# A decoder layer on one core: the per-layer embedding's projection moved from the routing to the place after the last expert

## The chip, the cores and the metric

The kernel runs on one core of a Trainium2 chip. The metric is the device time of one execution in microseconds (us). Lower is better. The core has a tensor engine (PE; PEld is its weight load), a vector engine (DVE), a scalar engine (ACT), a gather and scatter engine (POOL) and a queue engine (SP) that issues most of the transfers (DMAs).

## What is computed

One layer for 512 prompt tokens and 8 sample tokens (520 rows of 1024 numbers, float32):

```
h = x @ w_in                      # latents, rotary key, conv input, two gates
A = conv module,  B = latent attention, output projection to 1024
x = LN1(alpha*x + (sigmoid(gA)*A + sigmoid(gB)*B) @ w_out)
x = LN2(alpha*x + HierMoE(x))     # best of 4 groups, then best 2 of its 8 experts, SwiGLU
ple = sigmoid(x @ w_ple_gate) * (p @ w_ple_proj)      # p: 520 x 256, w_ple_proj: 256 x 1024
x = x + RMSNorm(ple) * ple_norm_g
```

The product `p @ w_ple_proj` is the per-layer embedding's projection. It depends on no other stage: its inputs are an input tensor and a weight. Only the last stage, called the tail here, reads its result.

## The kernel before

All engines work on one big SBUF tensor, `arena`, in which the offsets `A_...` give every buffer its place; `ps` is the PSUM with its eight banks of 512 columns. The program of each engine is written out by hand, in the order in which the engine executes it, and semaphores (`s_...`, `m....`) tie the engines together. Nothing reorders the work.

The rows are treated in five tiles: four of 128 rows and one of 8. `ORDER` (8-row tile first) is the order around the first layer norm, `ORDER2` (a full tile first, then the 8-row tile) the one in the tail. The program has these stages:

1. Input products, convolution, sample attention, prompt attention, output projection (up to line 1079).
2. Product with `w_out`, first layer norm on DVE, turning of each tile to `x1T` (`turn_x1`, L1085), and the routing's logits (`logits_x1`, L1095). The products with 36 columns go to bank 6.
3. Routing (L1930 to L2043): DVE finds the group and the experts, PE counts (L1142, L1144) and later places the tokens (L1156). `R_IDX` on the semaphore `s_r` says that the row indices are there. POOL then gathers the rows of the first block pair (L2203).
4. Experts: 18 passes over 16 pairs of experts. In each, `rows_in` turns the gathered rows (L1171), `gate_up` multiplies them with the two experts' weights (L1180), `turn_h` (L1187) and `down` (L1200) follow. The weights lie in three slots (`wx[0..2]`), which SP refills as they come free (L633): gate and up weights of pair k when the `gate_up` of the slot's last use is over (L668), down weights after its `down` (L674). POOL gathers rows and scatters results to DRAM (L2210).
5. A loop over experts that overflow (`overflow`, L549), which every engine runs through. Here no block overflows. When POOL is through, it raises `s_ovd` (L2241), and every engine waits for that.
6. Tail: SP loads the scattered results and the saved rows again (L708, L709). ACT scales each tile's first choice (`first_choice`, L1494), DVE adds up and normalizes (`front`: L2091, L2094 and `norm`, L1866 to L1876, with a root on ACT, L1499), PE turns the tile (`turn_x2`, L1240) and multiplies with `w_ple_gate` (L1265, L1273), ACT takes the sigmoid (L1514), DVE multiplies with the projection, and so on.

The projection is done by `ple_rows(u)` on PE (L1130), four products of 512 columns for a tile, which PE executes as eight MATMUL instructions since the data are float32. They go to banks 0 to 3, and ACT copies them to `x1` (`ple_out`, L1446), whose rows have been stored to DRAM by then. The calls stand between the steps of stages 2 and 3:

```
logits_x1(TILES - 2)
ple_rows(0)
turn_x1(TILES - 1)
logits_x1(TILES - 1)
ple_rows(1)
```

`ple_rows(2)` stands after the counting, `ple_rows(3)` and `ple_rows(4)` after the placing (L1156) and before the first `rows_in`, which also waits until ACT has emptied the banks. The weight `wpp` lies in the place of the buffer `yb` and is loaded by SP between the weights of slot 0 and of slot 1.

Of the kernel before, what the change touches and what calls it, by code (L numbers as in the profile page):

```python
# [14 lines left out]
P = 128  # L15
D = 1024
# [38 lines left out]
EW = EW1 + 2 * D  # L55
TILES = 5
ROWS = [P, P, P, P, NS]

ORDER = [4, 0, 1, 2, 3]
# [56 lines left out]
LN_STEPS, FD = 10, 8  # L116
# [80 lines left out]
A_W1 = A_OT  # L197
# [7 lines left out]
A_Y = A_W1 + 2 * EW  # L205
A_PLT = A_Y + 2048
assert A_PLT + 2 * T <= A_EXT
A_WPP = A_Y
A_PG = A_X1T

A_PLG = A_W1
A_ROWS = A_W1 + 8192
A_FX = A_W0
A_FBT = A_FX + TILES * D
A_SG = A_FBT + 2 * D
# [10 lines left out]
def decoder_layer(nc, a, o):  # L226

    ctx = ExitStack()
    with ctx:
# [7 lines left out]
        ps = ctx.enter_context(nc.psum_tensor("ps", [P, 8, 512], F32))  # L237
# [78 lines left out]
        wpp = at(A_WPP, 2 * D).rearrange("p (k n) -> p k n", k=2)  # L316
# [4 lines left out]
        plT = at(A_PLT, 2 * T).rearrange("p (k t) -> p k t", k=2)  # L321
# [142 lines left out]
        s_fd = sem("s_fd")  # L464
# [13 lines left out]
        s_plw = sem("s_plw")  # L478
        s_plg = sem("s_plg")
        s_pg = sem("s_pg")  # L480
        s_pp = sem("s_pp")
        s_ppe = sem("s_ppe")
# [78 lines left out]
        def _(sp):  # L561
# [75 lines left out]
                for x in range(2):  # L637
                    expert_weights(0, x, x, down)
            sp.wait_ge(s_mt, KD)
            sp.dma_start(wpp[:], a["w_plp"]).then_inc(s_plw, 16)  # L640
            sp.dma_start(plT[:], a["plT"]).then_inc(s_plw, 16)
            for down in range(2):
                for x in range(2):
# [35 lines left out]
            for k in range(3, EPAIRS):  # L679
# [5 lines left out]
                if k + 1 < EPAIRS and not early:  # L685
                    gate_up_weights(k + 1)
            sp.wait_ge(m.y, LAST_USE[EPAIRS - 3] + 1)
            sp.dma_start(plg[:], a["w_plg"]).then_inc(s_plg, 16)
            sp.dma_start(ln2r[:], a["lnrows"][:, 2:4]).then_inc(s_plg, 16)
            sp.wait_ge(s_r, R_STEPS)  # L690
# [14 lines left out]
            for u, t in enumerate(ORDER2):  # L705
                n = ROWS[t]
# [12 lines left out]
        def _(pe):  # L719
            mm = nc.tensor.matmul  # L720
# [380 lines left out]
            for u in range(1, TILES):  # L1101
                t, b = ORDER[u], 2 * (u % 2)
                if u >= 3:
                    pe.wait_ge(s_fd, FD * (u - 2) + 1)
                for k in range(KD):
# [4 lines left out]
                    for h in range(2):  # L1110
                        y = mm(ps[:, b + h, :], mixT[:, k, t * P:(t + 1) * P], wbig[:, k, h * 512:(h + 1) * 512],  # L1111
                               start=(k == 0), stop=(k == KD - 1))
# [1 line left out]
                if u >= 2:  # L1114
                    logits_x1(u - 2)
                turn_x1(u - 1)
            def ple_rows(u):

                t, b = ORDER[u], 2 - 2 * (u % 2)
                n = ROWS[t]  # L1120
                if u == 0:
                    pe.wait_ge(s_plw, 32)
                    pe.wait_ge(s_fd, FD * 3 + 1)
                elif u == 1:
                    pe.wait_ge(s_fd, FD * 4 + 1)
                else:
                    pe.wait_ge(s_ppe, u - 1)
                for k in range(2):
                    for h in range(2):
                        y = mm(ps[0:n, b + h, :], plT[:, k, t * P:t * P + n], wpp[:, k, h * 512:(h + 1) * 512],  # L1130
                               start=(k == 0), stop=(k == 1))
                y.then_inc(s_pp, 1)

            logits_x1(TILES - 2)
            ple_rows(0)
            turn_x1(TILES - 1)
            logits_x1(TILES - 1)
            ple_rows(1)


            pe.wait_ge(s_r, R_RANK)
            mm(ps[:, 7, 0:(TILES + 1) * 32], utri, ohs6.rearrange("p t e -> p (t e)"), start=True, stop=False)  # L1142
            for t in range(TILES):
                y = mm(ps[:, 7, 32 * (t + 1):32 * (TILES + 1)], ones, ohs[:, t:t + 1].to_broadcast([P, TILES - t, 32]),  # L1144
                       start=False, stop=(t == TILES - 1))
            y.then_inc(s_rp, 1)
            ple_rows(2)


            pe.wait_ge(s_rt2, 1)  # L1150
            for k in range(2):
                for t in range(TILES):
                    n = ROWS[t]
                    pe.wait_ge(s_rb, TILES * k + t + 1)
                    for x in range(2):
                        y = mm(ps[64 * x:64 * x + 64, 6, 0:SLOTS // P], inrow[0:n, k, t],  # L1156
                               inblk[0:n, k, t].rearrange("p (q x) -> p x q", x=2)[:, x],
                               start=(k == 0 and t == 0), stop=(k == 1 and t == TILES - 1))
            y.then_inc(s_rp, 1)


            ple_rows(3)
            ple_rows(4)

            def rows_in(p, xs, gathered):
                pe.wait_ge(s_xg[xs], gathered)
# [36 lines left out]


            pe.wait_ge(s_r, R_IDX)
            pe.wait_ge(s_ppe, TILES - 1)
            rows_in(0, 0, 16)
            pe.wait_ge(s_ppe, TILES)
            for p, (b, k) in enumerate(PASS):
                slot, n = weight_slot(k)  # L1210
                gate_up(p, slot, 32 * n)
# [2 lines left out]
                if p > 0:  # L1214
                    slot, n = weight_slot(PASS[p - 1][1])
# [17 lines left out]
            def turn_x2(u):  # L1233
                t = ORDER2[u]
                n = ROWS[t]
                pe.wait_ge(s_hf, HF_STEPS * (u + 1))
                if u >= 1:
                    pe.wait_ge(s_hc, 2 * u)
                for k in range(KD):
                    y = tr(ps[:, 4 + k // 4, (k % 4) * P:(k % 4) * P + n], fx[0:n, t, k * P:(k + 1) * P], ident[0:n, 0:n])  # L1240
                y.then_inc(s_ht, 1)

            pe.wait_ge(s_plg, 32)
            turn_x2(0)
            for u, t in enumerate(ORDER2):
                b = 2 * (u % 2)
                pe.wait_ge(s_hc, 2 * (u + 1))
                if u >= 2 and u != 3:
                    pe.wait_ge(s_hg, u - 1)
                if u == 1:  # L1250
                    narrow(6, lambda k: fbT[:, 1, k, 0:32], plg).then_inc(s_np, 1)
                elif u < TILES - 1:
                    for k in range(KD):
                        if k == KD // 2 and u == 0:
                            turn_x2(1)
                        if k == KD // 2 and u == 2:
                            pe.wait_ge(s_npc, 1)
                            narrow_sum(2, nparts, 1).then_inc(s_h, 1)
                            turn_x2(3)
                        if k == KD // 2 and u == 3:  # L1260
                            turn_x2(4)
                        if k == 0 and u == 3:
                            pe.wait_ge(s_hg, 2)
                        for h in range(2):
                            y = mm(ps[:, b + h, :], fbT[:, u % 2, k], plg[:, k, h * 512:(h + 1) * 512],  # L1265
                                   start=(k == 0), stop=(k == KD - 1))
                    y.then_inc(s_h, 1)
                    if u == 0:
                        turn_x2(2)
                else:  # L1270
                    for h in range(2):
                        for k in range(KD):
                            y = mm(ps[:, b + h, :], fbT[:, u % 2, k], plg[:, k, h * 512:(h + 1) * 512],  # L1273
                                   start=(k == 0), stop=(k == KD - 1))
                        y.then_inc(s_h, 1)
# [3 lines left out]
        def _(act):  # L1279
# [158 lines left out]

            def ple_out(u):

                t, b = ORDER[u], 2 - 2 * (u % 2)
                n = ROWS[t]
                act.wait_ge(s_pp, u + 1)
                act.wait_ge(s_fx, u + 1)
                act.wait_ge(s_x1[u], 16)
                av(x1[0:n, t], ps[0:n, b:b + 2, :].rearrange("p h n -> p (h n)"), ACT.Copy).then_inc(s_ppe, 1)  # L1446

            ple_out(0)
            x1_out(TILES - 1)

            act.wait_ge(s_r, R_EXP)
            av(gg[:], gx[:], ACT.Exp).then_inc(s_ra, 1)
            act.wait_ge(s_r, R_EXP2)
            av(gf, gf, ACT.Exp).then_inc(s_ra, 1)
            for u in range(1, TILES):
                ple_out(u)

            def rows_in(p):
                act.wait_ge(m.xt, p + 1)
# [56 lines left out]
            def squares(u):  # L1516
# [3 lines left out]
                act.wait_ge(s_hs, 2 * u + 1)  # L1520
                av(rms[0:n, 1:2], rms[0:n, 0:1], ACT.Sqrt, bias=eps[0:n, 0:1], scale=1.0 / D).then_inc(s_hs, 1)

            act.wait_ge(s_ovd, 1)
            for u in range(3):
                first_choice(u)
# [839 lines left out]
```

## Time and profile before

| | |
|---|---|
| median of 3 runs | 1042.96 us (1040.09 to 1043.85) |
| the profiled execution: its own time | 1042.33 us |
| span in its profile | 1040.6 us |
| PE busy | 937.9 us (90% of the span) |
| DVE, ACT, POOL busy | 422.9, 244.1, 94.4 us |
| moved by the DMAs | 244.08 MB, mean 235 GB/s |
| chain of work that ended last | PE 72%, DMA 14%, DVE 8%, ACT 3%, the rest queues and issue |

The span is what the profiler sees between the first and the last instruction; the execution's own time has 1.7 us around it. "Busy" says that an engine works on an instruction. It does not say that the time hangs on it: this is read from the chain of work that ended last, which goes back from the last instruction to what released it each time. The granted clock (PEclk) is 1.00 where TensorE has its 2.4 GHz and 0.50 where it has 1.2 GHz.

### The profile page before, as it was taken

Reading aid. Unit: us, or ns where it says so; the run is one execution under the profiler, and the core shown is the slowest. Engines: PE = TensorE matmul, PEld = TensorE weight load, DVE = VectorE, ACT = ScalarE, POOL = GpSimd, SP = SyncE. Lnnn points to the kernel's source line nnn. Section 1 sums busy time; section 2 is a strip of 40 time slices with the busy share of each in tenths; the row PEclk is TensorE's granted clock in tenths of the full one; section 3 lists DMA queues with packets and bytes.
Section 4 is the critical chain, followed back from the end, with each engine's and each line's share of the span. In section 5 each row is a group of like instructions: output and inputs, shape, how many; then the busy total and the mean of one; then the engine's idle time right before and its main releaser. Section 6 shows DMA issues by size and latency. Waiting matters only on the chain.

```text
span 1040.6 us, 13802 instructions
## 1 busy us (share of the span) xinstructions
PE 937.9 (90%) x5204; PEld 562.2 (54%) x5204; DVE 422.9 (41%) x934; ACT 244.1 (23%) x515; POOL 94.4 (9%) x143
## 2 busy tenths in 40 slices
PE   7999988999989989999899998889999987950996
PEld 6777766777767755665588444443333332320442
DVE  0211387565543247668512344452111111113773
ACT  0122121032224015766600000211111110101344
POOL 0111211211112000000000000011111111110000
PEclk9999998999999999999999999889999998995899
DMA  9766885996967500101125942329999999977001
GB/s 377 283 232 244 308 298 200 319 349 236 361 224 249 225 26 19 44 20 38 66 102 222 423 205 106 137 72 409 425 419 427 422 423 426 408 307 251 1 21 61
DMA packets 61221, 244.08 MB, mean 235 GB/s; under 512 B 10738, under 2 KB 11507, under 8 KB 51683
## 3 DMA queue, kind: packets, MB, share of 16 engines
q1 hardware_dynamic: 42818, 189.04, 46.6%
q0 software_dynamic: 13152, 35.28, 9.4%
q10 hardware_dynamic: 5184, 18.88, 4.8%
q8 instruction: 42, 0.69, 0.3%
q14 instruction: 25, 0.20, 0.1%
HBM read 239.69 MB, written 14.87 MB: 245 GB/s over the span
## 4 chain that ended last, share of the span: by engine, by line
PE 72%; DMA 14%; DVE 8%; ACT 3%; issue 2%; SPq 1%; ACTq 0%; DVEq 0%; POOLq 0%
PE ps L768 17%; DMA arena<-in_wexp 10%; PE ps L1180 8%; PE ps L1068 5%; PE ps L1111 5%; PE ps L1265 3%; PE ps L1200 3%; PE ps L856 3%; PE ps L761 3%; PE ps L827 3%; PE ps L937 2%; DMA arena<-in_state 2%; DVE arena L1747 2%; PE ps L961 2%; PE ps L1130 1%
## 5 line engine op out<-in xcount | busy, mean ns | idle before, releaser
L768 PE MATMUL ps<-arena 128*128 128x260 f32 x960 | 223.7, 389 | 6.1 <-DMA arena<-in_w 6.1
L768 PEld LDWEIGHTS ps<-arena 128*128 128x128 f32 x960 | 181.4, 193 | 40.7 <-issue 8.5
L1180 PE MATMUL ps<-arena 128*64 128x512 f32 x576 | 129.4, 602 | 16.0 <-DMA arena<-in_wexp 14.5
L1180 PEld LDWEIGHTS ps<-arena 128*64 128x64 f32 x576 | 42.7, 139 | 90.3 <-issue 88.4
L1599 DVE SCALAR_TENSOR_TENSOR arena<-arena,vec 128x512 f32<-128x512 f32 x120 | 81.9, 745 | 0.0
L2169 POOL DMA_DIRECT2D arena<-in_kv x96 | 51.7, 539 | 285.9 <-issue 279.8
L1200 PE MATMUL ps<-arena 128*64 128x512 f32 x288 | 65.8, 598 | 3.8 <-DMA arena<-in_wexp 3.0
L2053 DVE TENSOR_TENSOR arena<-ps,arena 128x256 f32<-128x256 f32 x18 | 7.6, 425 | 140.2 <-ACT arena L1464 140.2
L1068 PE MATMUL ps<-arena 128*128 128x260 f32 x256 | 56.3, 383 | 0.7 <-issue 0.7
L1111 PE MATMUL ps<-arena 128*128 128x512 f32 x128 | 56.1, 595 | 0.0
L1068 PEld LDWEIGHTS ps<-arena 128*128 128x128 f32 x256 | 48.7, 191 | 8.2 <-issue 1.0
L1265 PE MATMUL ps<-arena 128*128 128x512 f32 x96 | 43.9, 614 | 1.2 <-ACT arena L1505 1.2
L1111 PEld LDWEIGHTS ps<-arena 128*128 128x128 f32 x128 | 24.0, 190 | 29.9 <-issue 29.9
L1200 PEld LDWEIGHTS ps<-arena 128*64 128x64 f32 x288 | 19.6, 137 | 37.7 <-issue 36.7
L1464 ACT ACTIVATE arena<-ps 128x256 f32<-128x256 f32 x18 | 6.9, 383 | 138.8 <-PE ps L1180 138.8
L856 PE MATMUL ps<-arena 128*32 128x256 f32 x512 | 32.7, 398 | 7.2 <-DVE arena L1618 7.2
L937 PE MATMUL ps<-arena 128*128 128x128 f32 (+3 forms) x128 | 38.1, 441 | 0.0
L1606 DVE TENSOR_REDUCE peak<-ps 128x1 f32<-128x512 f32 x16 | 11.1, 691 | 64.3 <-PE ps L831 64.3
L1381 ACT ACTIVATE arena<-arena,nb 128x128 f32<-128x128 f32 (+1 forms) x64 | 36.0, 562 | 2.1
L2203 POOL DMA_INDIRECT arena<-x_scratch,idx x20 | 20.3, 1013 | 172.1 <-PE ps L1171 132.1
L1240 PE MATMUL ps<-con,arena 128*128 128x128 f32 (+1 forms) x40 | 5.8, 291 | 32.9 <-DVE arena L1876 32.9
L2063 DVE COPY arena<-ps 128x512 f32<-128x512 f32 x18 | 12.5, 692 | 55.9 <-PE ps L1200 55.9
(307 smaller groups left out, 1138.1 us busy)
## 6 DMA issues: line engine op xcount, KB each, us to landing
arena<-in_wexp SPq DMA_DIRECT2D x32, 2048.0 KB, 23.6
arena<-in_kv SPq DMA_DIRECT2D x160, 272.0 KB, 8.8
arena<-in_wexp SPq DMA_DIRECT2D x32, 1024.0 KB, 25.8
arena<-in_kv POOLq DMA_DIRECT2D x96, 272.0 KB, 7.0
arena<-in_w ACTq DMA_DIRECT2D x36, 512.0 KB, 7.0
arena<-in_wo SPq DMA_DIRECT2D x8, 512.0 KB, 3.8
arena<-in_w_out SPq DMA_DIRECT2D x4, 1024.0 KB
arena<-in_w_plg SPq DMA_DIRECT2D x1, 4096.0 KB, 15.0
```

Source lines behind the costliest of these rows:

```text
L761: y = mm(ps[:, b + h, 0:TH], w[:, KC * (j % 2) + k], aT[:, k, h * TH:(h + 1) * TH], start=(k == 0), stop=(k == KC - 1))
L768: y = mm(ps[:, b + h, 0:TH], w[:, k], xT[:, k, h * TH:(h + 1) * TH], start=(k == 0), stop=(k == KD - 1))
L856: y = mm(ps[32 * bb:32 * bb + 32, 7, 0:KVL], pts[:, s, u * P + 32 * bb:u * P + 32 * bb + 32], kvr[:, s, bb, u, 2 * P + 32:REC], start=(u = ...
L937: y = mm(ps[:, bank, c0:c0 + (i + 1) * P], qT[:, p % 4, x, i * P:(i + 1) * P], kT[:, s, x, 0:(i + 1) * P], start=True, stop=True)
L1068: y = mm(ps[:, 2 * s + h, 0:TH], wo[s][:, k], oT[:, k, h * TH:(h + 1) * TH], start=(k == 0), stop=(k == KD - 1))
L1111: y = mm(ps[:, b + h, :], mixT[:, k, t * P:(t + 1) * P], wbig[:, k, h * 512:(h + 1) * 512], start=(k == 0), stop=(k == KD - 1))
L1180: y = mm(ps[64 * x:64 * x + 64, 2, :], xgT[:, k, 64 * x:64 * x + 64], wx[slot][:, x, k * 512:(k + 1) * 512], start=(k == 0), stop=(k == KD ...
L1200: y = mm(ps[64 * x:64 * x + 64, 6 + h, :], htT[:, c, 64 * x:64 * x + 64], wx[slot][:, x, o0:o0 + 512], start=(c == 0), stop=(c == 1))
L1265: y = mm(ps[:, b + h, :], fbT[:, u % 2, k], plg[:, k, h * 512:(h + 1) * 512], start=(k == 0), stop=(k == KD - 1))
L1381: av(q, q, ACT.Exp, bias=nb[:, x, i:i + 1], scale=SCALE, accum_out=rs[:, x, i:i + 1]).then_inc(s_ex, 1)
L1599: y = v.scalar_tensor_tensor(out=aT[:, c, 0:NPR], in0=win, scalar=wt, in1=aT[:, c, 0:NPR], op0=ALU.mult, op1=ALU.add)
L2169: pool.dma_start(rec[:, n % 2, SPN + j], a["kv"][bass.ds(pg, 1)].rearrange("a p n -> (a p) n")).then_inc(s_kvp[n % 2], 16)
```

## The change

All five calls of the projection are taken out of stages 2 and 3. They now stand on PE after the wait for `s_ovd` and before the first `turn_x2`, that is, between the last expert's `down` and the tail. ACT's five `ple_out` stand at the head of its tail, ahead of `first_choice`. The weight `wpp` gets a place in slot 1 behind the tail's other weights, and SP loads it (1024 KB) when slot 1 is free for good, just ahead of the gate weight `plg`. The waits on `s_ppe` before the first expert pass go away.

```
-A_WPP = A_Y
+A_WPP = A_ROWS + 2 * D
...
             sp.wait_ge(s_mt, KD)
-            sp.dma_start(wpp[:], a["w_plp"]).then_inc(s_plw, 16)
             sp.dma_start(plT[:], a["plT"]).then_inc(s_plw, 16)
...
             sp.wait_ge(m.y, LAST_USE[EPAIRS - 3] + 1)
+            sp.dma_start(wpp[:], a["w_plp"]).then_inc(s_plw, 16)
             sp.dma_start(plg[:], a["w_plg"]).then_inc(s_plg, 16)
...
             logits_x1(TILES - 2)
-            ple_rows(0)
             turn_x1(TILES - 1)
             logits_x1(TILES - 1)
-            ple_rows(1)
...
-            ple_rows(2)
...
-            ple_rows(3)
-            ple_rows(4)
...
             pe.wait_ge(s_r, R_IDX)
-            pe.wait_ge(s_ppe, TILES - 1)
             rows_in(0, 0, 16)
-            pe.wait_ge(s_ppe, TILES)
...
+            pe.wait_ge(s_plw, 32)
+            for u, t in enumerate(ORDER):
+                b, n = 2 * (u % 2), ROWS[t]
+                if u >= 2:
+                    pe.wait_ge(s_ppe, u - 1)
+                for k in range(2):
+                    for h in range(2):
+                        y = mm(ps[0:n, b + h, :], plT[:, k, t * P:t * P + n], wpp[:, k, h * 512:(h + 1) * 512],
+                               start=(k == 0), stop=(k == 1))
+                y.then_inc(s_pp, 1)
             pe.wait_ge(s_plg, 32)
             turn_x2(0)
+            pe.wait_ge(s_ppe, TILES)
...
-            ple_out(0)
             x1_out(TILES - 1)
...
-            for u in range(1, TILES):
-                ple_out(u)
...
+            for u in range(TILES):
+                ple_out(u)
             act.wait_ge(s_ovd, 1)
             for u in range(3):
                 first_choice(u)
```

Three places show the order of the instructions. First, PE around the last tile's logits and the counting, before (L1095 logits, L1130 projection, L1085 turning of a tile, L1142 and L1144 counting; a row counts products; the profile shows two instructions for each, turnings apart):

```order
L1095 MATMUL ps<-arena 128x36 x8
L1130 MATMUL ps<-arena 8x512 x4
L1085 MATMUL ps<-con,arena 128x128 x8
L1095 MATMUL ps<-arena 128x36 x8
L1130 MATMUL ps<-arena 128x512 x4
L1142 MATMUL ps<-arena,con 128x192
L1144 MATMUL ps<-arena,con 128x160
```

After the change (the same lines are L1096, L1086, L1125 and L1127):

```order
L1096 MATMUL ps<-arena 128x36 x8
L1086 MATMUL ps<-con,arena 128x128 x8
L1096 MATMUL ps<-arena 128x36 x8
L1125 MATMUL ps<-arena,con 128x192
L1127 MATMUL ps<-arena,con 128x160
```

The groups of the projection ahead of the last tile's turning and behind its logits are gone. Second, PE from the end of the counting to the first expert pass, before (L1156 placing, L1171 turning of the gathered rows, L1180 the first `gate_up`):

```order
L1144 MATMUL ps<-arena,con 128x32
L1130 MATMUL ps<-arena 128x512 x4
L1156 MATMUL ps<-arena 64x26 x20
L1130 MATMUL ps<-arena 128x512 x8
L1171 MATMUL ps<-con,arena 128x128 x8
```

After the change (L1127, L1138, L1151, L1160):

```order
L1127 MATMUL ps<-arena,con 128x32
L1138 MATMUL ps<-arena 64x26 x20
L1151 MATMUL ps<-con,arena 128x128 x8
L1160 MATMUL ps<-arena 64x512 x16
L1151 MATMUL ps<-con,arena 128x128 x8
```

Three groups are gone here, and the turning of the first expert rows follows the placing directly. Third, ACT at the head of the tail, before (L1494 first choices, L1499 the root):

```order
L1494 ACTIVATE arena<-arena,gates 128x1024
L1494 ACTIVATE arena<-arena,gates 8x1024
L1494 ACTIVATE arena<-arena,gates 128x1024
L1499 ACT_TABLE_LOAD
L1499 ACTIVATE rstd<-mv,eps 128x1
L1505 ACTIVATE arena<-ps 128x512 x2
```

After the change (L1436 the copies of the projection, L1481, L1486):

```order
L1436 ACTIVATE arena<-ps 8x1024
L1436 ACTIVATE arena<-ps 128x1024 x4
L1481 ACTIVATE arena<-arena,gates 128x1024
L1481 ACTIVATE arena<-arena,gates 8x1024
L1481 ACTIVATE arena<-arena,gates 128x1024
L1486 ACT_TABLE_LOAD
L1486 ACTIVATE rstd<-mv,eps 128x1
```

Five copies, each of which waits for PE's projection of its tile, now stand ahead of the first choices.

## Rows read from the trace of the kernel before

**Rows 1.** Chain of waits, 640 us to the end, around the routing: start us, us, what

```profile
650.47 3.60 PE ps L1095 x16
654.06 5.10 PE ps L1130 x8
659.17 1.04 PE ps L1085 x8
...
661.36 1.99 PE ps L1095 x16
...
669.26 0.59 PE ps L1142 x2
669.85 1.11 PE ps L1144 x10
...
682.83 9.61 PE ps L1130 x16
692.43 0.89 PE ps L1171 x8
...
694.36 7.09 PE ps L1180 x32
```

**Rows 2.** Timeline of ACT, 640 to 705: start us, us, engine line op, shapes [idle before]

```profile
692.47 1.02 ACT L1446 ACTIVATE arena<-ps 128x1024 f32<-128x1024 f32 x1 [2.41 <-PE ps L1130]
```

**Rows 3.** Windows: us, busy of PE, PEld, DVE, ACT, POOL, PEclk, DMA share, GB/s

```profile
664.00:666.00 2.00, 2.00 (x4) 0.77 (x3) 1.86 (x17) 0.22 (x1) 0.00 (x0) 0.51 0.00 0
666.00:668.00 2.00, 2.00 (x5) 0.77 (x3) 1.86 (x20) 0.21 (x1) 0.00 (x0) 0.64 0.00 0
...
686.00:688.00 2.00, 2.00 (x4) 0.69 (x3) 1.90 (x4) 0.00 (x0) 1.12 (x2) 0.52 0.09 19
...
966.00:968.00 2.00, 2.00 (x4) 0.71 (x3) 1.93 (x3) 0.00 (x0) 0.00 (x0) 0.55 0.00 0
```

**Rows 4.** The first gather: POOL's timeline, then its landing in the DMA view

```profile
685.03 1.08 POOL L2203 DMA_INDIRECT arena<-x_scratch,idx  x1 [39.73 <-DVE arena L2024]
...
arena<-x_scratch,idx POOLq DMA_INDIRECT x1, 3.3
```

**Rows 5.** Windows of the experts' stage, columns as in rows 3

```profile
715.00:730.00 15.00, 15.00 (x74) 5.45 (x76) 3.16 (x6) 2.18 (x4) 3.06 (x3) 1.00 1.01 420
895.00:910.00 15.00, 13.28 (x66) 5.20 (x64) 2.14 (x4) 1.58 (x3) 2.64 (x3) 1.00 0.96 402
```

**Rows 6.** The same chain: a first product after a pause in the experts' stage

```profile
871.85 8.96 PE ps L1180 x32
```

**Rows 7.** The same chain: from the last expert to the tail's first product

```profile
926.59 3.68 PE ps L1200 x16
...
954.95 1.15 ACT arena L1494
...
961.41 1.95 PE ps L1240 x8
...
964.52 8.75 PE ps L1265 x16
```

**Rows 8.** POOL's release of `s_ovd`, line 2241: first and last start at the end

```profile
L2241 POOLq EVENT_SEMAPHORE  x1: 17/17/17, 935.8 to 935.8; - x1
```

**Rows 9.** Timeline of the tail's head, 945 to 960, columns as in rows 2

```profile
949.29 1.15 ACT L1494 ACTIVATE arena<-arena,gates 128x1024 f32<-128x1024 f32 x1 [18.40 <-DMA arena<-x_scratch]
...
954.48 0.21 DVE L1868 BATCH_NORM_AGGREGATE mv<-bst 128x2 f32<-128x12 f32 x1
...
956.11 1.28 ACT L1499 ACT_TABLE_LOAD   x1
957.41 0.29 ACT L1499 ACTIVATE rstd<-mv,eps 128x1 f32<-128x1 f32 x1
```

**Rows 10.** DMA view, 860 to 965: issues, KB each, median us to landing

```profile
arena<-in_w_plg SPq DMA_DIRECT2D x1, 4096.0 KB, 15.0
...
arena<-in_lnrows SPq DMA_DIRECT2D x1, 1024.0 KB, 27.8
```

More of the change, by code:

```diff
@@ L212 @@
 A_ROWS = A_W1 + 8192
+A_WPP = A_ROWS + 2 * D
+assert A_WPP + 2 * D == A_W1 + 2 * EW
 A_FX = A_W0
@@ L1116, in _ @@
                 turn_x1(u - 1)
[L1117 to L1132, printed above, removed]
             logits_x1(TILES - 2)
-            ple_rows(0)
             turn_x1(TILES - 1)
             logits_x1(TILES - 1)
-            ple_rows(1)
             pe.wait_ge(s_r, R_RANK)
@@ L1439, in ple_out @@
             def ple_out(u):
-                t, b = ORDER[u], 2 - 2 * (u % 2)
+                t, b = ORDER[u], 2 * (u % 2)
                 n = ROWS[t]
```

## The prediction

> **What bounds the kernel now.** I read four views in this order. The chain of waits gives what the end hangs on. Around the routing it alternates between PE and DVE, and two groups of the projection lie in it: eight instructions at 654.06 (5.10 us) and sixteen at 682.83 (9.61 us) [rows 1]. The other two groups are not in it, they lie under DVE's routing steps. The windows show the experts' stage bound by transfers: from 715 to 730 us and still from 895 to 910 the DMA engines are 1.01 and 0.96 busy [rows 5], and the chain goes through waits for expert weights. That stream of weights starts when the first `gate_up` ends (694.36 + 7.09 = 701.45) [rows 1], so what the first pass gains, the whole stage gains. At the end PE is through with the experts at 930.27, and its next piece in the chain starts at 961.41 [rows 7]: over 31 us with an idle PE, under the last scatter and the reload of the results. The timeline shows who sets the first turning there: the first choices, the adds and the root [rows 9]. The last view is the granted clock [rows 3], since every pause in this program brings it down to 0.50.
>
> **The change, part one: the routing.** Removing the first group takes 5.10 us from the path [rows 1]. It also takes away the work under which the clock came up again. The logits at 650.47, behind a pause and at the low level by their length, take 3.60 us, the same sixteen instructions at 661.36, at the high level, 1.99; the turning of a full tile takes 1.04 at the high and 1.95 at the low level [rows 1, 7]. Without the group the turning and the last logits come straight behind work at the low level. I take both as low: +0.91 and +1.61. The net gain there is 5.10 - 2.52 = 2.58 us.
>
> The second and third group were covered by DVE's steps: nothing gained. But the counting (0.59 + 1.11 = 1.70 us) [rows 1] follows a pause now and runs at the low level. The two pairs above give factors 1.81 and 1.88; with 1.85 it costs +1.45. The placing was at the low level before and stays there. So the indices come 2.58 - 1.45 = 1.13 us earlier.
>
> The last two groups (9.61 us) ended at 692.43. Without them the first turning of expert rows waits for the gather: it is issued at 685.03 and lands 3.3 us later, at 688.33 [rows 4]; moved by 1.13 this is 687.20, 5.23 before 692.43. So of the 9.61 us at most 4.1 were on the path, the rest lay over the gather. PE has paused then, and the turning costs 0.91 more. For the first pass the nearest row is the one at 871.85, also after a pause: 8.96 us in place of 7.09 [rows 1, 6], +1.87. Sum of part one: -5.23 + 0.91 + 1.87 = **-2.45 us** at the end of the first `gate_up`. As the transfers bind from there on, I carry it unchanged to the last expert. The bounds are the case in which the clock doesn't suffer (-9.2, below) and the case in which nothing of it comes through (0).
>
> **Part two: the place before the tail.** PE may start when POOL raises `s_ovd`, at 935.8 [rows 8]. I work with the old times and add part one at the end. Forty instructions: sixteen took 9.61 us, with the clock low for their first 5.1 us (up at 687.9: 0.52 from 686 to 688) [rows 1, 3], so 7.06 at the high level, 0.44 each, and forty take 17.6. Three times the clock stayed low under work: from 664.0 to 667.4 (0.51 from 664 to 666, 0.64 from 666 to 668), from 682.8 to 687.9 and from 964.5 to 967.8 (0.55 from 966 to 968) [rows 3, 7]: 3.4, 5.1 and 3.3 us, mean 3.9. Half of that is lost: +2.0. PE ends at 935.8 + 19.6 + 0.1 = 955.5, and ACT's last copy (1.02) [rows 2] at 956.6. PE is not held by the two pairs of banks, since a copy is far shorter than the 3.5 us of a group.
>
> Only then does ACT reach the first choices. Before, it began them at 949.29, and DVE had the statistics at 954.48 + 0.21 = 954.69, 5.40 us later [rows 9]. Now that is 956.6 + 5.4 = 962.0. ACT itself needs three choices of 1.15 and a table load of 1.28 before the root: free at 961.4, just in time. The root starts at 962.0, where it started at 957.41 before [rows 9]: **+4.6 us**. It is less than the 7.3 us by which the choices are late, because before the third choice waited for its data until 954.95 and the root stood behind it [rows 7, 9]; this stall vanishes. All that follows the root is the same work in the same order. Its first turning and product ran at the low level and do so again, since PE pauses from 955.5 to 966.0; the product had its clock back after 3.3 us, the shortest of the three, so I add (3.9 - 3.3) / 2 = 0.3.
>
> The Trainium skill, ScalarE: Activation LUTs, section What ACT_TABLE_LOAD costs, says that a switch of the table costs a drain of 1.38 us besides the load, 2.66 in all. The row shows the root 1.30 us after the load began, with no drain behind it [rows 9]. By the page ACT would be free at 962.8 and the time 0.8 us longer than my sum; the trace disagrees and I go by it.
>
> **Part three: the transfers.** 1024 KB less are loaded before the first expert, where PE and not the queue binds: zero. The same 1024 KB are issued now at 911.2 (old time), behind the last expert weights and ahead of the gate weight, whose landing took 15.0 us and that of the rows behind it 27.8 [rows 10]. It delays no expert weight. It may push the scatter and the reload by its own length, 2.4 us at the 420 GB/s of the stage [rows 5]; the cover is that the first choices begin 7.3 us later than before and the third one only at 958.9, when even 954.95 + 2.4 is over. That is zero too, and without this cover it would cost up to 2.4.
>
> **Sum:** -2.45 + 4.6 + 0.3 = +2.45 us. Against the profiled execution (1042.33) this is 1044.8; the median of the runs lies 0.63 higher, and on it I get 1045.4, which is my forecast: +0.23%. A measurement here can tell about 0.5% (5.2 us) from no change, so I forecast no change.
>
> **The rivals.**
> *The projection waits for its weight (slower).* PE's first product waits for `wpp` too. It was under way 15.0 us as the gate weight was, landing at 926.2, in time. But the rows behind needed 27.8, to 939.0 [rows 10]. If the new load lands like those, PE starts 3.2 us late and everything behind with it: +5.65 us, 1048.6, slower by over 0.5%. It decides from a landing 27.4 us after the issue on. For it speaks only that row; against it that `wpp` is issued first. The Trainium skill, DMA: Bandwidth & Descriptors, section Two DMAs through the same engine are not ordered, says that a queue starts its descriptors in order but promises no order of completion. By it the weight could land as late as the last of them.
>
> *The gain of the routing is lost.* If the stream of weights does not end earlier though it starts earlier (its rate varies), only the tail's part is left: +4.9, 1047.9, at the border. For it: single windows are 0.90 to 1.01 busy. Against it: the chain has no wait that is pinned to anything but that stream and PE.
>
> *The clock stays high in the pauses.* Then part one is 5.10 for the first group, and the first turning is at 683.2 instead of 692.4: -9.2 us. With the tail as forecast it is -4.3, 1038.7; with the clock up there too (-2.3) it is 1036.4, faster by over 0.5%. For it: the work from 653.9 on did bring the clock up, and the new turning stands there in its place. Against it: the low stretches of [rows 3] follow a pause or the logits, and the turning at 961.41 (1.95 us) did not lift the clock before the product behind it [rows 3, 7]. The Trainium skill, TensorE: Matmul & The Clock Gate, section HAM oscillation — how this bites in real kernels, says that waits between bursts let the clock fall back, so that each burst starts slow. It speaks against filler being taken out of the routing: by it the gain is my 2.45, without it 9.2.
>
> That the change does not do what it says is excluded by the order of the instructions: the five groups are gone from the routing and stand ahead of the tail.
>
> **How the numbers follow.** Forecast 0.62, its own range 1042 to 1049 (clock phases of 1 us each, the spread of the runs); weight late 0.13; gain lost 0.13; clock high 0.12. Slower by over 0.5%: 0.08 from the late weight, 0.06 from the lost gain, 0.07 from the forecast's upper end, 0.21. Faster: a third of the clock case, 0.04. Same: 0.75. The range from 1040 to 1050 leaves out the larger part of the clock case and a tenth above.
>
> **What would show it.** The last logits end some 2.6 us earlier and take 3.6 us; the counting takes about 3.1; the first gather is issued near 683.9 and the first turning starts near 687.2; the first pass takes 8.5 to 9.5. In the tail the forty instructions take 19 to 20 us from the release of `s_ovd`, and the first choice begins at once after the fifth copy. From the last `down` to the first turning it is 35.7 us instead of 31.1. I am wrong if PE waits for `wpp`, if the turning and the last logits take 1.0 and 2.0 us, if the weights' stage is longer than before, or if the root waits for the table load.

## The result, and the profile after

The changed kernel takes 1048.76 us (median of 6 runs, 1047.44 to 1053.16), the kernel before 1041.36 in the same comparison. The ratio is 1.0077, with a 95% interval from 1.0051 to 1.0103: slower, by 7.4 us by the medians and 8 by the ratio. A second comparison gave 1.0068 [1.0044, 1.0093], 7 us. The forecast was 2.45 us more, 1045.4, and "no change", with the border set at 0.5% (5.2 us). The measured change is beyond that border, an outcome to which the prediction gave a chance of 0.21. The time lies in its range of 1040 to 1050, 1.2 us below the upper end: the range was wide enough, the size does not fit.

One thing has to be known to read the profiles: in both kernels some runs are about 4 us longer than the others, and the profiled run of the changed kernel (1053.04) is one of those, that of the kernel before is not. In that profile the extra time lies ahead of 530 us, in code that the change does not touch: the granted clock is 0.93 from 350 to 400 us and 0.97 from 480 to 530, where the kernel before has 0.97 and 1.00. So all stretches below are counted from an instruction behind that, the second last logits, at 650.47 before [rows 1] and at 654.61 here. Counted so, the profile after is not 10.7 but 6.6 us longer.

The chain of waits of the changed kernel around the routing (start us, us, what) answers to [rows 1]:

```profile
654.61 3.60 PE ps L1096 x16
658.21 1.77 PE ps L1086 x8
...
661.14 3.65 PE ps L1096 x16
...
670.68 1.01 PE ps L1125 x2
671.69 2.09 PE ps L1127 x10
...
691.24 1.95 PE ps L1151 x8
...
694.64 9.53 PE ps L1160 x32
```

The group of 5.10 us between the logits and the turning is gone, and turning, last logits and counting all run at the low level: 1.77, 3.65, and 1.01 + 2.09 in place of 1.04, 1.99, and 0.59 + 1.11. The first turning of expert rows starts 36.6 us after the second last logits, where it was 42.0. The first pass takes 9.53 us where it took 7.09. It ends at 704.17, 49.56 after the logits; before it was 50.98 after them. The granted clock says the same: it is 0.50 in every window read from 656 to 698 us, so the routing runs at the low level from end to end.

The same chain at the end answers to [rows 7]:

```profile
917.23 8.78 PE ps L1160 x32
...
930.56 3.68 PE ps L1180 x16
...
939.77 1.33 issue
941.10 19.64 PE ps L1229 x40
...
961.68 1.15 ACT arena L1481
...
971.11 1.95 PE ps L1218 x8
...
974.32 9.68 PE ps L1255 x16
```

From the end of the last `down` (934.24) to the first turning of the tail it is 36.9 us, before 31.1. This stretch has three parts now: PE starts the projection 6.9 us after the `down`, the forty instructions take 19.6, and the turning starts 10.4 after them. POOL's release and PE's own branches in the overflow loop (columns: least, median and longest ns, first and last start) are these:

```profile
L2230 POOLq EVENT_SEMAPHORE  x1: 17/17/17, 939.7 to 939.7; - x1
```

```profile
L555 PEldq COMPARE_BRANCH  x8: 215/215/5087, 931.8 to 940.5; - x8
```

The release is at 939.7, but one of PE's eight branches (`PEldq`, the queue with PE's weight loads) took 5.1 us, so PE was through its loop only at 941. Before, none took over 0.36 us. The DMA view answers to [rows 10]:

```profile
arena<-in_w_plg SPq DMA_DIRECT2D x1, 4096.0 KB, 17.8
...
arena<-in_w_plp SPq DMA_DIRECT2D x1, 1024.0 KB, 17.2
arena<-in_lnrows SPq DMA_DIRECT2D x1, 1024.0 KB, 29.8
```

The projection's weight was there 17.2 us after its issue (913.52), at 930.7, well ahead of PE.

### The profile page after: what moved, and what is told of

It is laid out like the page before. It is cut to its first block, busy times and chain, and to the rows that moved or that the text cites. A ratio compares the mean times of both kernels' runs of the same rounds, so it can differ in the third digit from the quotient of the medians.

```text
span 1051.3 us, 13802 instructions
## 1 busy us (share of the span) xinstructions
PE 948.0 (90%) x5204; PEld 566.4 (54%) x5204; DVE 422.8 (40%) x934; ACT 243.8 (23%) x515; POOL 94.4 (9%) x143
## 4 chain that ended last, share of the span: by engine, by line
PE 73%; DMA 12%; DVE 8%; ACT 3%; issue 3%; SPq 1%; POOLq 0%; ACTq 0%; DVEq 0%; POOL 0%
PE ps L769 17%; DMA arena<-in_wexp 10%; PE ps L1160 9%; PE ps L1069 5%; PE ps L1112 5%; PE ps L1255 4%; PE ps L1180 3%; PE ps L857 3%; PE ps L762 3%; PE ps L828 3%; PE ps L938 2%; DMA arena<-in_state 2%; PE ps L1229 2%; DVE arena L1736 2%; PE ps L962 2%
## 5 line engine op out<-in xcount | busy, mean ns | idle before, releaser
L1160 PE MATMUL ps<-arena 128*64 128x512 f32 x576 | 134.8, 623 | 16.4 <-DMA arena<-in_wexp 14.5
L1160 PEld LDWEIGHTS ps<-arena 128*64 128x64 f32 x576 | 43.9, 143 | 95.1 <-issue 92.6
L1180 PE MATMUL ps<-arena 128*64 128x512 f32 x288 | 65.7, 598 | 2.1 <-DMA arena<-in_wexp 1.3
L1180 PEld LDWEIGHTS ps<-arena 128*64 128x64 f32 x288 | 19.6, 136 | 36.0 <-issue 35.1
L1752 DVE CUSTOM_DVE_ANT_0 arena<-ps,con 128x128 f32<-128x128 f32 (+1 forms) x64 | 28.0, 487 | 10.3 <-PE ps L938 10.0
```

The source lines that it names most:

```text
L1160: y = mm(ps[64 * x:64 * x + 64, 2, :], xgT[:, k, 64 * x:64 * x + 64], wx[slot][:, x, k * 512:(k + 1) * 512], start=(k == 0), stop=(k == KD ...
L1180: y = mm(ps[64 * x:64 * x + 64, 6 + h, :], htT[:, c, 64 * x:64 * x + 64], wx[slot][:, x, o0:o0 + 512], start=(c == 0), stop=(c == 1))
```

## The experiments

Each run is timed beside the kernel before, on the same chip. Its profile is read in four stretches: from the second last logits to the end of the first `gate_up`; from there to the end of the last `down` (the stage); from there to the first turning of the tail; and from there to the end of the span. The table is worked out from the chains and timelines of each profile (a start plus its duration, less the other). The medians and the ratio with its interval come from all runs; the first median is that of the kernel, the second that of the kernel before beside it.

| kernel | to first pass | stage | to the tail's turning | to the end | medians | ratio |
|---|---|---|---|---|---|---|
| before | 50.98 | 228.8 | 31.2 | 79.2 | | 1 |
| before, 2nd profile | 50.72 | 228.5 | 28.1 | 79.1 | | |
| before, 3rd profile | 50.87 | 228.8 | 30.1 | 79.7 | | |
| changed | 49.56 | 230.0 | 36.9 | 80.2 | 1048.76, 1041.36 | 1.0077 [1.0051, 1.0103] |
| changed, 2nd profile | 49.03 | 230.2 | 36.6 | 80.1 | 1048.23, 1041.41 | 1.0068 [1.0044, 1.0093] |
| no projection | 49.61 | 230.4 | 29.8 | 80.2 | 1041.71, 1041.82 | 1.0002 [0.998, 1.0025] |
| projection at both places | 50.98 | 231.2 | 36.4 | 80.6 | 1051.43, 1041.82 | 1.0074 [1.0049, 1.0099] |
| behind the last `down` | 49.24 | 230.0 | 30.4 | 79.9 | 1042.59, 1041.82 | 1.0012 [0.9991, 1.0032] |
| the same, again | 49.35 | 230.2 | 30.4 | 79.8 | 1042.33, 1041.41 | 1.0018 [0.9998, 1.0037] |
| changed, idle products in the pauses | 47.10 | 230.4 | 36.0 | 80.4 | 1046.27, 1041.82 | 1.0036 [1.0014, 1.0058] |
| spread over the pauses | 45.87 | 230.2 | 31.8 | 80.5 | 1040.43, 1041.41 | 0.9988 [0.9969, 1.0008] |
| the same, DVE's copy first | 44.69 | 231.2 | 28.6 | 79.4 | 1037.92, 1041.41 | 0.9972 [0.9951, 0.9993] |

**Each part alone.** First the changed kernel without any projection:

```
-            pe.wait_ge(s_plw, 32)
-            for u, t in enumerate(ORDER):
...
-            for u in range(TILES):
-                ple_out(u)
...
-            dve.wait_ge(s_ppe, TILES)
+            dve.wait_ge(s_plw, 32)
```

> The changed kernel without the projection: its forty products and five copies are left out, the embedding's part of the output is not computed. It shows part one (the routing without the groups) alone. My account of the changed kernel's trace: the routing gains 1.4 us up to the first gate_up, the experts' stage gives 1.2 back, the tail is that of the kernel before: 1041 us, within 0.2% of the kernel before. Rival 'the routing's part is worth its forecast': 2.5 us faster. Rival 'the loss is made in the routing, by the low clock': 3 us or more slower, 1044 or above.

It is as fast as the kernel before (1.0002). Taking the projection out of the routing altogether, where it kept PE busy for some 24 us, and putting it nowhere, is worth nothing that can be measured: against the mean of the three profiles of before it gains 1.2 us in the first stretch, and gives back 1.7 in the stage and 0.8 behind the turning. Nothing more is to be had from part one as it stands, without another edit in the routing. The rival that makes the loss there falls as well.

Then the other part alone: the kernel before, with all its groups, and the projection done again at the new place.

```
+            sp.dma_start(wpl[:], a["w_plp"]).then_inc(s_plw, 16)
             sp.dma_start(plg[:], a["w_plg"]).then_inc(s_plg, 16)
...
+            pe.wait_ge(s_plw, 48)
+            for u, t in enumerate(ORDER):
...
+            for u in range(TILES):
+                act.wait_ge(s_pp, TILES + u + 1)
...
             act.wait_ge(s_ovd, 1)
```

> The kernel before with its projection in the routing kept, and the same projection done a second time at the place of the change (the weight loaded a second time there). It shows the tail's part alone. If the whole loss is the forty products between the release by POOL and the first choices: 5 to 7 us slower than before (1046.5 to 1048.5). Rival 'the tail costs only the forecast 4.9': 1046. Rival 'most of the loss comes from the routing': under 3 us slower.

The ratio, 1.0074, is that of the change, though the routing is the one of before. The median, 1051.43, is above the expected 1046.5 to 1048.5: by the medians the kernel is 9.6 us slower, by the stretches 10.5. Of these 6.6 us lie between the last `down` and the turning (36.4 less the mean of 29.8 in three profiles of before), which is the loss that comes with the new place. The stage takes 2.5 us more and the part behind the turning 1.3, of which more below. The timeline of PE in this run (start us, us, line, shapes, idle before):

```profile
929.41 3.65 PE L1204 MATMUL ps<-arena 128*64 128x512 f32 x16 [0.75 <-DVE arena L2077]
938.67 20.42 PE L1254 MATMUL ps<-arena 128*8 128x512 f32 x40 [5.60 <-POOLq L2261]
969.48 1.94 PE L1244 MATMUL ps<-con,arena 128*128 128x128 f32 x8 [10.39 <-DVE arena L1896]
```

Here PE is released by POOL without a late branch, 5.60 us after the `down`, and the turning comes 36.4 us after it, as in the changed kernel. The forty instructions take 20.4. The zero of this sum is the wait for the reload in the kernel before. Its first turning of the tail starts 31.2 us after the `down` in the first profile, and 28.1 and 30.1 in the two others:

```profile
957.56 1.94 PE L1240 MATMUL ps<-con,arena 128*128 128x128 f32 x8 [28.06 <-DVE arena L1876]
```

```profile
960.41 1.94 PE L1240 MATMUL ps<-con,arena 128*128 128x128 f32 x8 [30.09 <-DVE arena L1876]
```

**The place, not the work.** The same forty instructions and five copies ahead of the overflow loop and not behind the wait for POOL:

```
             down(NPASS - 1, slot, 32 * n)
+            pe.wait_ge(s_plw, 32)
+            for u, t in enumerate(ORDER):
...
             overflow(pe, blocks, extra)
             pe.wait_ge(s_ovd, 1)
...
-            pe.wait_ge(s_plw, 32)
-            for u, t in enumerate(ORDER):
...
             rows_out(NPASS - 1, 1, 16 * (NPASS // 2 - 1))
+            for u in range(TILES):
+                ple_out(u)
```

> The changed kernel with the forty products and five copies ahead of the overflow loop, directly behind the last down, not behind the wait for POOL. If the cost of the tail is that the products start 6.9 us after the last down and end after the results have been reloaded, they now run from the end of the last down at the high clock for 17.6 us, end about when the first choices' data arrive (15.0 us after the reload's start), and the time is within 1.5 us of the kernel before: 1040 to 1042.5, 6 to 8 us below the changed kernel. Rival 'the weight then comes too late' (it landed 17.2 us after its issue, 3.5 us before the last down ended): up to 3 us more. Rival 'the loss lies in the routing': still 1046 or above.

Its chain of waits:

```profile
926.32 3.65 PE ps L1180 x16
929.98 17.48 PE ps L1205 x40
947.47 0.47 ACT arena L1437
...
950.96 1.16 ACT arena L1484
...
960.40 1.96 PE ps L1229 x8
```

PE goes from the last `down` into the projection without a pause, so the clock stays high and forty instructions take 17.5 us. The last copy starts at 947.47, and the first choice follows once ACT is through its own loop, at 950.96. The median is 1042.59 and the ratio 1.0012 with an interval that holds 1. Of the 7 to 8 us of the change some 6 are gone with the same lines in another place: 36.9 and 36.6 us from the `down` to the turning became 30.4. The weight was in time: issued at 909.25 and landed 17.3 us later, 3.4 us before PE wanted it. The same kernel again, in a second comparison:

> The projection directly behind the last down once more, unchanged, as a control on the same chip as the runs above: the same as before within 0.3%, 1040 to 1043.5, and 3 to 4 us above the version with the groups in the pauses, if the pauses are worth anything.

It gave 1.0018, in line; the margin to the version with the groups spread over the pauses (below) was 2 us by the medians (1042.33 and 1040.43), less than expected. Both intervals just hold 1, and both ratios lie above it: a cost of 1 to 2 us is not excluded.

**The clock in the routing.** The changed kernel with four groups of idle products in the pauses:

```
+            def fill(g):
+                for k in range(2):
+                    for h in range(2):
+                        mm(ps[:, 2 * (g % 2) + h, :], plT[:, k, 0:P], plT[:, k, 0:512], start=(k == 0), stop=(k == 1))
...
             logits_x1(TILES - 1)
+            fill(0)
...
             y.then_inc(s_rp, 1)
+            fill(1)
+            fill(2)
...
+            fill(3)
             pe.wait_ge(s_r, R_IDX)
             rows_in(0, 0, 16)
```

> The changed kernel with four groups of four idle products (into free banks, read by nobody) in the routing's pauses: one behind the last logits, two behind the counting, one ahead of the gather's wait. It shows what the clock is worth there. If the low clock eats the routing's gain: counting back to 1.7 us, the first turning to about 1.0 and the first pass to 7.1 to 8; 3 to 5 us below the changed kernel (1044 to 1046). Rival 'the clock is of no account there': the same as the changed kernel, 1048 to 1049.

The first pass ended 2.5 us earlier than in the first profile of the changed kernel and 1.9 earlier than in the second, since the counting took 1.7 us in place of 3.1 and the first turning 1.06 in place of 1.94. The median was 1046.27: work that nobody reads made the kernel some 2 to 3 us faster (1.0036 beside 1.0077 and 1.0068; the intervals overlap a little, and PE had no late branch here, which is worth up to 1.3). But the first pass still took 8.78, outside the expected 7.1 to 8, and the timeline of all engines shows a new wait in front of it:

```profile
685.92 1.06 PE L1161 MATMUL ps<-con,arena 128*128 128x128 f32 x8 [0.50 <-DMA arena<-x_scratch,idx]
...
687.02 0.60 ACT L1458 ACTIVATE arena<-ps 128x512 f32<-128x512 f32 x1 [21.08 <-PE ps L1161]
...
688.45 0.16 DVE L2043 TENSOR_TENSOR gates<-gates,arena 128x5 f32<-128x5 f32 x1
...
688.64 0.69 DVE L2049 COPY arena<-ps 128x512 f32<-128x512 f32 x1
...
689.44 3.16 PE L1170 MATMUL ps<-arena 128*64 128x512 f32 x8 [2.45 <-issue]
```

PE has turned the rows by 686.98 and ACT copies its half at once. DVE copies the other half only at 688.64, when the last of its routing steps (`gates`, 688.45) is over. PE waits 2.45 us, some 1.7 of them for that copy, and the clock falls again, to 0.50 from 690 to 692. The changed kernel has the same wait, shorter, since its turning is later:

```profile
693.64 0.17 DVE L2032 TENSOR_TENSOR gates<-gates,arena 128x5 f32<-128x5 f32 x1
...
693.84 0.69 DVE L2038 COPY arena<-ps 128x512 f32<-128x512 f32 x1
...
694.64 1.98 PE L1160 MATMUL ps<-arena 128*64 128x512 f32 x4 [1.46 <-ACT arena L1447]
```

**What the two findings give together.** The projection in pauses where nothing waits for it: the 8-row tile's group behind the last logits and not ahead of the turning, two behind the counting, one ahead of the gather's wait, and the last one directly behind the last `down`.

```
             logits_x1(TILES - 2)
-            ple_rows(0)
             turn_x1(TILES - 1)
             logits_x1(TILES - 1)
-            ple_rows(1)
+            ple_rows(0)
...
+            ple_rows(1)
             ple_rows(2)
...
             ple_rows(3)
-            ple_rows(4)
...
             down(NPASS - 1, slot, 32 * n)
+            ple_rows(TILES - 1)
```

> The projection's groups put where nothing waits for them: the 8-row tile's behind the last logits, two behind the counting, one ahead of the gather, the last one behind the last down (its weight loaded a second time). If the routing's 5.1 and 9.6 us on the path can be had with the clock kept up, the first pass ends 3.5 to 4 us earlier than before (47 us after the second last logits, as with the idle products), the tail is as before: 3 to 4 us faster than before, 1037.5 to 1039. Rival 'the ACT copies and waits in the pauses eat it': within 1 us of before.

The first pass ends 5.0 us earlier than in the kernel before, more than expected, and takes 7.09 us, though PE waits 2.60 us ahead of it:

```profile
689.19 7.09 PE L1183 MATMUL ps<-arena 128*64 128x512 f32 x32 [2.60 <-DVE arena L2054]
```

But the time falls by no more than 1.2 us by the ratio, and the interval holds 1. Of the 5.0 the stage gave back 1.5, the tail's wait for its data 2.0 and its first product 1.2 (all against the mean of three profiles of before, in which that wait alone varies by 3.1). The median missed the expected 1037.5 to 1039. Then the same with DVE's copy of the first rows ahead of its last eleven steps:

```
             assert count[0] == R_IDS, count
...
+            rows_in(0)
...
-            rows_in(0)
             for p in range(NPASS):
                 hidden(p)
```

> The same, and DVE copies the first expert rows ahead of its last eleven routing steps, not behind them. In the run with idle products PE waited 1.8 us for that copy. If DVE's queue is what bounds the first pass there, it starts 1.4 to 1.8 us earlier and the time falls by as much below the run without this edit: 4.5 to 5.5 us below before. Rival 'the gather binds': no difference between the two.

The chain of this run at the first pass:

```profile
690.17 0.89 PE ps L1174 x8
...
691.15 0.70 DVE arena L2038
...
692.10 7.09 PE ps L1183 x32
```

DVE's copy follows the turning at once. The first stretch is 1.2 us shorter, less than the 1.4 to 1.8 expected, and the median is 1037.92 beside 1041.41: 0.9972, with an interval below 1. That is 3 us, not the expected 4.5 to 5.5. It beats both kernels, by 3 us over before and 10 over the change. That the copy did it is shown for the first stretch alone: the intervals of the two versions overlap, and most of what its profile is shorter than the one above, 3.2 us, lies in the tail's wait for its data, which varies by as much in the kernel before.

**Chance or not.** The changed kernel again, and the kernel before twice:

> The changed kernel once more, for a second profile. In the first one PE began the forty products 1.3 us after POOL's release, since one branch of its own loop had taken 5.1 us, and the experts' stage had taken 230.1 us against 228.8 before. If both are chance, the branch takes 0.2 to 0.4 us here, PE starts within 0.2 us of the release, and the stage differs from 230.1. If they come with the change, both are seen again. Ratio again 1.005 to 1.010.

> The kernel before, for a second profile. The one shown had an experts' stage of 228.8 us (end of the first gate_up to the end of the last down) and a first product of the tail of 8.75 us; seven other profiles had 230.0 to 231.2 and 8.9 to 10.1. If the short stage and product are chance, this one has 229.5 to 231.5 and 9 to 10; if they belong to the kernel before, 228.8 and 8.8 again, and then the change lengthens the stage by 1.3 us.

> A third profile of the kernel before, for the same question; the same numbers are expected as of the second.

The ratio of the repeated comparison is 1.0068, as expected. The late branch is no chance: 5.13 us in the second profile of the changed kernel (its PE began at 936.41, 1.3 us after the release at 935.1), 4.59 in the one without projection, 0.36 in all other kernels. So it comes with these two programs; what in them makes it was not tried. The stage is no chance either: 228.5 to 228.8 in three profiles of before, 230.0 to 231.2 in all the others. The chains show where. The last expert weights land 212.9 to 213.4 us after the first pass in all kernels but the last version (214.1). The difference lies in the last pass behind them, which PE enters after a pause of 3.4 us in each of them. PE's timeline in the kernel before:

```profile
914.95 7.09 PE L1180 MATMUL ps<-arena 128*64 128x512 f32 x32 [3.40 <-DMA arena<-in_wexp]
```

And in the kernel with the projection at both places:

```profile
915.00 9.86 PE L1184 MATMUL ps<-arena 128*64 128x512 f32 x32 [3.40 <-DMA arena<-in_wexp]
```

In three profiles of before the clock stayed high over that pause and the pass took 7.09; in all nine others it took 8.67 to 9.86. The clock does not fall at the same moment in them: in the kernel with both places it is at 0.95 in the last 2 us of the pause (912 to 914) and at 0.50 from 914 on, in the changed kernel it is still at 1.00 from 916 to 918 and at 0.51 from 918 to 920, under work. The kernel with both places has the routing of before and enters the pass at the same time. Up to this pass one thing alone that it executes is new, apart from where things lie in the program and in the memory: the load of the projection's weight, 3.7 us ahead of it:

```profile
911.27 0.35 SPq L691 DMA_DIRECT2D arena<-in_w_plp  x1
```

All the other kernels, even the one without projection, have this load too, just ahead of the last pass, and the kernel before has not. It does not delay the expert weights. Whether it is what brings the clock down there was not tried: that would take the kernel before with this load and nothing else. It is not the only thing that can: one of the passes in the middle of the stage (at 801.60 us before, behind a wait of 2.3) took 7.09 us in all profiles with the routing of before and 8.71 or 8.78 in all others, some 110 us ahead of that load. Why the clock falls ahead of the last pass stays open.

The first product of the tail is a weaker case: 8.75, 8.67 and 9.24 us in the three profiles of before, 8.91 to 10.11 in the others. The two overlap, so that it comes with the change is not shown.

## Why the prediction was right and where it was wrong

**The routing's first half was right.** The turning, the last logits and the counting run at the low level, within 0.2 us of what was written. The first turning of expert rows was forecast 36.73 us after the second last logits and came after 36.63 and 36.70.

**The first pass was taken too short.** Forecast -2.45 us for part one; the two profiles show -1.56 on the mean of three of before, 0.9 less. Three terms were too small. The copy between turning and pass was counted as before, but DVE is in its last routing steps then, and PE waits 1.46 and 1.39 us instead of 1.05: 0.4. I had moved PE's work forward without asking what stands ahead of the copy on DVE. The pass itself cost 9.53 and 9.0 for the 8.96 of [rows 6]: 0.3 in the mean. The turning took 1.95 where 0.89 and 0.91 had been added: 0.15.

**"I carry it unchanged to the last expert" failed.** The stream of weights did carry it, to within half a microsecond: this part of the step was right, and the rival of the lost gain had the wrong reason. But behind the stream, the last pass takes 1.7 us more. The whole stage is 1.4 us longer than before, which is one of the signs of being wrong that the prediction names. With that, nothing is left of part one, as the run without any projection shows. The prediction's ground for the clock was too wide: that every pause in this program brings it down does not hold even in the profile it was read from. There PE waited 2.28, 3.04, 1.72 and 3.40 us at 801.60, 836.73, 899.49 and 914.95, and what followed ran at the high level (7.09 us for a pass, 3.65 for a `down`); behind 7.11 us, at 871.85, it did not.

**The tail: the length was right, what it was set against was not.** The forty instructions were forecast at 19.6 us and took 19.64 and 19.29. ACT's copies, the choices and the root followed as written, and the table load was no bound: it began at 964.91 and took 1.28, and the root followed at 967.11, directly behind DVE's statistics. The Trainium skill (ScalarE: Activation LUTs, What ACT_TABLE_LOAD costs) counts a drain of 1.38 us besides the load, in all 2.66 us. With both of them behind the load's start the root could not have run before 967.57, so the trace speaks against it here. From `down` to turning the forecast was 35.7; measured were 36.9 and 36.6, and the late branch explains it: PE started 6.9 us after the `down`, and 5.6 where no branch was late (the kernel with both places and the one with idle products). The larger error is on the other side. The kernel before had 31.2 us there in the one profile at hand, and 28.1 and 30.1 in two more, since it waits there for the reload, whose landing varies. The changed kernel does not wait for data there any more, and its 36.9 and 36.6 lie close together. Against the mean of 29.8 the cost is 6.9 us and not 4.6. Of the 2.3 us between them 1.3 are this zero: one profile's wait was taken for that of the kernel.

**The sum.** Against the means of the profiles: first pass -1.6, stage +1.4, tail +6.9, first product and the rest +0.8, in all 7.6 us, as measured (7.4 by the medians). Forecast were -2.45, 0, +4.6 and +0.3. All four errors go the same way, and none of the rivals is what happened. That the time still lies in the range owes more to the width of the range than to the sum.

**The rivals.** Two of them come close in time, the late weight with 1048.6 and the lost gain with 1047.9 for the measured 1048.76, but neither for its reason. The stream of weights did end earlier, as it began earlier. The weight was not late: it was the first of its queue's three and landed 17.2 us after its issue, where 27.4 would have decided. What the Trainium skill says of the order of completion (DMA: Bandwidth & Descriptors, Two DMAs through the same engine are not ordered) was not called on; the three landed in the order of their issue, the last after 29.8. The clock did not stay high in the pauses. The page on the clock gate (the Trainium skill, TensorE: Matmul & The Clock Gate, HAM oscillation — how this bites in real kernels) agrees with the rows of the routing: with the filler gone each burst there started at 1.2 GHz (granted clock 0.50), and with idle products put back the counting returned to 1.7 us. The waits in the experts' stage named above, after which work went on at the high level, show that not every wait does this.

## What to carry to other kernels

Independent work that fills a pause is free only where its end comes before what the pause waits for; ask that of the engine, and of every engine that must empty its result. Here the same forty instructions cost 1 to 2 us by the ratios when started with the end of the last `down`, which could not be told from nothing, and 7 to 8 us when started behind a wait for another engine that they did not need. A stretch that waits for a transfer varies from run to run, and one profile is a poor zero to count from: take it from several, above all where the change ends the dependence on that transfer. And when a step is pulled forward, look at what stands ahead of its successor on each other queue, not only at the one it left.

## What the runs showed of the hardware

A branch on PE's sequencer, of the loop over experts that overflow, took 5.1 us in two profiles of one program and 4.6 in a near relative, and 0.36 at the longest in all programs with other code around it. After the same pause of 3.4 us ahead of the last pass, the clock stayed at 2.4 GHz in three of three profiles of the kernel before and fell to 1.2 GHz in all nine profiles of the seven other kernels, for a cost of 1.6 to 2.8 us (8.67 to 9.86 us for the pass in place of 7.09). Idle products of which nobody reads the result gained 1.9 to 2.5 us in the routing.
